# Reversed column order in the products that hold the weights in the array

## The reference

```python
for i in range(2):
    a = _rmsnorm(h, norm_mix[i])
    y = _mla(a, ...) if i == 0 else _swa_sinks(a, ...)       # each: h @ w_in, attention, @ w_o
    h = h + y
    h = h + _conv_ffn(_rmsnorm(h, norm_ffn[i]), ffn_w_in[i], ffn_conv_w[i], ffn_conv_b[i], ffn_w_out[i])
return _rmsnorm(h, final_norm)

def _conv_ffn(h, w_in, conv_w, conv_b, w_out):               # w_in 2048 x 11264, w_out 5632 x 2048
    u = h @ w_in
    c = conv_b + sum(shifted(u, j) * conv_w[j] for j in range(3))
    gate, val = jnp.split(c, 2, axis=-1)
    return (jax.nn.silu(gate) * val) @ w_out
```

## Time and profile before

| | value |
|---|---|
| median of three runs | 2016.89 us (2015.31 to 2018.02) |
| the profiled execution's own time | 2015.52 us |
| its span, first to last instruction | 2013.4 us |
| mean granted TensorE clock | 0.997 |
| PE busy | 1984.8 us, 99% |
| DVE busy | 1424.3 us, 71% |
| ACT busy | 988.0 us, 49% |
| from HBM | 364.94 MB, 185 GB/s in the mean |

### The profile page before, as it was taken

One profiled execution on the slowest core, in us unless ns is written; L12 is line 12 of the kernel. 1 busy time (PEld: TensorE's weight loads), 2 busy tenths in 40 slices (PEclk: granted clock), 3 DMA queues, 4 the chain that ended last, 5 costly groups with the idle time before them and its releaser, 6 DMA issues.

```text
span 2013.4 us, 33994 instructions
## 1 busy us (share of the span) xinstructions
PE 1984.8 (99%) x12104; PEld 1767.9 (88%) x12104; DVE 1424.3 (71%) x1964; ACT 988.0 (49%) x1159; POOL 146.3 (7%) x147
## 2 busy tenths in 40 slices
PE   8999999999999999999999999999999999999998
PEld 7898888888888888888899888888888888888887
DVE  7766687887787877554566668778787877855554
ACT  6456445555555554434355554555555555533332
POOL 1112220000000000110120004100000000001110
PEclk9999999999999999999999999999999999999999
DMA  7556555555555565556675335655556555555553
GB/s 280 160 195 157 180 197 190 192 181 197 191 185 177 192 202 189 188 179 202 191 242 174 126 127 168 199 192 183 179 193 201 188 180 199 185 197 189 189 188 115
DMA packets 103881, 374.48 MB, mean 186 GB/s; under 512 B 11547, under 2 KB 12124, under 8 KB 103548
## 3 DMA queue, kind: packets, MB, share of 16 engines
q1 hardware_dynamic: 101180, 362.55, 54.4%
q0 software_dynamic: 2624, 10.83, 2.1%
HBM read 364.94 MB, written 8.39 MB: 185 GB/s over the span
## 4 chain that ended last, share of the span: by engine, by line
PE 91%; DVE 4%; issue 0%; ACT 0%; DVEq 0%; ACTq 0%
PE ps L409 53%; PE ps L412 28%; PE ps L694 2%; PE ps L695 1%; PE ps L696 1%; DVE w_lo L1111 1%; DVE scores_b L1500 1%; PE ps L732 1%; PE ps L743 1%; PE ps L755 1%; PE ps L440 1%; PE ps L439 1%; PE ps L438 1%; DVE cv L1126 0%; PE ps L513 0%
## 5 line engine op out<-in xcount | busy, mean ns | idle before, releaser
L1111 DVE TENSOR_TENSOR w_lo<-raw,w_hi 128x1024 fp32r<-128x1024 f32 (+1 forms) x682 | 830.6, 1231 | 503.5 <-ACT w_hi L825 482.3
L825 ACT ACTIVATE w_hi<-raw 128x1024 fp32r<-128x1024 f32 (+1 forms) x682 | 715.2, 1055 | 792.3 <-PE ps L412 593.7
L409 PE MATMUL ps<-op_in,w_hi 128*128 128x512 f32 x2992 | 1028.2, 391 | 9.5 <-DVE w_lo L1111 9.5
L412 PE MATMUL ps<-op_in,w_lo 128*128 128x256 f32 x2992 | 813.0, 282 | 0.0
L409 PEld LDWEIGHTS ps<-op_in,w_hi 128*128 128x128 f32 x2992 | 549.7, 188 | 113.8 <-issue 8.4
L412 PEld LDWEIGHTS ps<-op_in,w_lo 128*128 128x128 f32 x2992 | 565.7, 189 | 15.7
L409 PE MATMUL ps<-op_ffn,w_hi 128*128 128x512 f32 x1408 | 486.2, 390 | 0.0
L412 PE MATMUL ps<-op_ffn,w_lo 128*128 128x256 f32 x1408 | 391.7, 282 | 0.0
L409 PEld LDWEIGHTS ps<-op_ffn,w_hi 128*128 128x128 f32 x1408 | 262.2, 188 | 53.0
L412 PEld LDWEIGHTS ps<-op_ffn,w_lo 128*128 128x128 f32 x1408 | 266.0, 189 | 2.7
L1616 POOL TENSOR_TENSOR cg<-h 128x1024 f32 (+1 forms) x15 | 43.2, 2877 | 1604.9 <-DVE h L1364 1454.3
(11 more groups left out here) (203 smaller groups left out, 1663.5 us busy)
## 6 DMA issues: line engine op xcount, KB each, us to landing
raw<-weights SPq DMA_DIRECT2D x666, 512.0 KB, 3.4
raw<-weights SPq DMA_DIRECT2D x16, 384.0 KB, 3.2
bias_rows<-brow POOLq DMA_DIRECT2D x1, 6144.0 KB, 36.7
win_bias<-bias_rows POOLq DMA_DIRECT2D x4, 1024.0 KB, 8.6
h<-xt SPq DMA_DIRECT2D x8, 256.0 KB, 7.7
x_tok<-x_rows SPq DMA_DIRECT2D x2, 1024.0 KB, 10.3
y<-yt SPq DMA_DIRECT2D x4, 512.0 KB, 4.0
par<-params SPq DMA_DIRECT2D x1, 352.0 KB, 11.5
```

The costliest lines, as they stand in the source:

```text
L409: return mm(ps[:, bank, 0:2 * T], whi, op, start=start, stop=stop)
L412: return mm(ps[:, bank, 0:T], wlo, op[:, 0, :], start=False, stop=False)
L825: f(w_hi[s][:, 0:cols], raw[s][:, 0:cols], ACT.Copy).then_inc(hi_ready, 1)
L1111: v.tensor_tensor(w_lo[s][:, 0:cols], raw[s][:, 0:cols], w_hi[s][:, 0:cols].bitcast(F32), ALU.subtract).then_inc(lo_ready, 1)
```

## The change

All products with stationary weights (L409 and L412, L513 to L515, L694 to L696) read the columns of their moving operand with a step of -1, from the last to the first, and write the PSUM columns with a step of -1 as well, so that each result lands where it did. In a wide product the two parts of the operand are taken as one run of 512 columns, and that run is reversed. Number, shape, order, buffers and waits of the instructions of every engine stay as they are; the line numbers behind L409 go up by one.

```diff
                 def high():
-                    return mm(ps[:, bank, 0:2 * T], whi, op, start=start, stop=stop)
+                    return mm(ps[:, bank, 0:2 * T][:, ::-1], whi, op.rearrange("p a t -> p (a t)")[:, ::-1],
+                              start=start, stop=stop)
 
                 def low():
-                    return mm(ps[:, bank, 0:T], wlo, op[:, 0, :], start=False, stop=False)
+                    return mm(ps[:, bank, 0:T][:, ::-1], wlo, op[:, 0, :][:, ::-1], start=False, stop=False)
...
-                            o = ps[:, b0 + m // 2, m % 2 * T:(m % 2 + 1) * T]
-                            mm(o, w_hi[s][:, w], x[:, 0, :], start=c == 0 and kt == 0 and m != 1, stop=False)
-                            mm(o, w_lo[s][:, w], x[:, 0, :], start=False, stop=False)
-                            z = mm(o, w_hi[s][:, w], x[:, 1, :], start=False, stop=c == 1 and kt == 1 and m != 0)
+                            o = ps[:, b0 + m // 2, m % 2 * T:(m % 2 + 1) * T][:, ::-1]
+                            mm(o, w_hi[s][:, w], x[:, 0, :][:, ::-1], start=c == 0 and kt == 0 and m != 1, stop=False)
+                            mm(o, w_lo[s][:, w], x[:, 0, :][:, ::-1], start=False, stop=False)
+                            z = mm(o, w_hi[s][:, w], x[:, 1, :][:, ::-1], start=False, stop=c == 1 and kt == 1 and m != 0)
...
-                    o = ps[:, bank + j // 2, j % 2 * T:(j % 2 + 1) * T]
+                    o = ps[:, bank + j // 2, j % 2 * T:(j % 2 + 1) * T][:, ::-1]
...
-                        mm(o, w_hi[s][:, w], op[:, kt0 + k, 0, :], start=first and k == 0 and j % 2 == 0, stop=False)
-                        mm(o, w_lo[s][:, w], op[:, kt0 + k, 0, :], start=False, stop=False)
-                        z = mm(o, w_hi[s][:, w], op[:, kt0 + k, 1, :], start=False, stop=last and k == 1 and j % 2 == 1)
+                        mm(o, w_hi[s][:, w], op[:, kt0 + k, 0, :][:, ::-1], start=first and k == 0 and j % 2 == 0, stop=False)
+                        mm(o, w_lo[s][:, w], op[:, kt0 + k, 0, :][:, ::-1], start=False, stop=False)
+                        z = mm(o, w_hi[s][:, w], op[:, kt0 + k, 1, :][:, ::-1], start=False, stop=last and k == 1 and j % 2 == 1)
```

## The result

The changed kernel takes 2037.82 us (median of 4 runs, 2036.15 to 2039.31), the kernel before 2016.2 us (4 runs, the profiled one among them): a ratio of 1.0103, interval 1.009 to 1.0115. It is 21.6 us slower. I had forecast no change, at 2016.5 us; the time lies within the range of 1990 to 2065 us and on the side of a rival.

A forecast was written before the change was run, and what follows sets the result against it. The prediction took PE (TensorE) as the bound, with 1850 of 2013.4 us in edited products. All four items summed to 0 on the profiled 2015.52 us; with the runs' median 1.4 us above, it forecast 2016.5 us, range 1990 to 2065.

The forecast's parts named there:

- no change: Whole kernel: the reversed products cost nothing more or less, about 2016.5 us, 2012 to 2021 in this case; chance 0.55.
- What bounds the kernel: PE, busy 99% of the span: any nanosecond added to or taken from an edited product is one of the program.
- Item 1: Moving operand of the edited products read downwards: taken as 0, since a jump of read address costs at most 1 ns.
- Item 2: PSUM written downwards by the edited products: taken as 0, between wide bounds of 5230 us loss and 45 us gain.
- Item 3: Distance between a PSUM write and the add on it, 256 columns instead of 512 within a wide tile: price 0.
- Item 4: Load of the next product's weights: unchanged, might hide some ns at 4848 + 1440 products, none at the wide ones.
- The doubled column: Rival: in reversed products each column is handled alone and takes twice its time, 3820 us in all; chance 0.15.
- The fixed price per product: Rival: each reversed product costs a few ns more, 2028 us at 1 ns, 2061 us at 4 ns; chance 0.15.
- Less stalling: Rival: weight loads and moving reads meet less in memory, 1971 us if all 4 ns go, 1994 at half; chance 0.15.
- the 4 ns besides the columns: Time a product of 256 columns holds beside its columns, 0.117 - 0.113 us; by 11136 products, 45 us of possible gain.

The follow-up runs named there:

- experiment 3: Kernel before, wide tiles read and written downwards, but the wide product takes its two halves in the usual order: 2036.39 us, ratio 1.0097.
- read_down: Kernel before, only the moving operand of both wide-tile products read downwards, PSUM written upwards: 2037.58 us, ratio 1.0103.
- write_down: Kernel before, only the PSUM outputs of both wide-tile products written downwards, operand read upwards: 2017.63 us, ratio 1.0001.
- halves_down: The run of experiment 3: kernel before, wide tiles downwards, the wide product's halves in the usual order: 2036.39 us, ratio 1.0097.
- experiment 6: Kernel before, all reads upwards, wide tiles take their weights 8 columns (32 bytes) further on: 2045.29 us, ratio 1.014.
- experiment 4: Kernel before, only the wide product of the wide tiles turned round, in operand and PSUM: 2046.41 us, ratio 1.0147.
- experiment 7: Kernel before, only the narrow product of the wide tiles turned round, in operand and PSUM: 2015.76 us, ratio 0.9993.
- up_off160: Kernel before, upward reads, operand tiles placed 128 bytes further on: 2018.51 us in one run, beside 2018.26 us for the kernel before.
- up_off0: Kernel before, upward reads, operand buffers at 0 instead of 32 modulo 128 bytes: 2046.29 us, ratio 1.0141.
- up_w32: The run of experiment 6: kernel before, upward reads, wide tiles' weights taken 32 bytes further on: 2045.29 us, ratio 1.014.
- low_down: The run of experiment 7: kernel before, only the narrow product of the wide tiles turned round: 2015.76 us, ratio 0.9993.

## Why the prediction was wrong, point by point

*What bounds the kernel* was right: each added ns of a wide tile came out in the span, and nothing hid it.

*Item 1, the downward read taken at 0*, is the step that failed. Its size is 4.3 ns a wide tile of `f0_out` and 1.1 ns a product of the narrow tiles, 20.1 us of the program from the 501st product on. I took the bound from L438, whose operand with a hole costs no more than one without. The jump is indeed free (experiment 3), but that row says nothing of a direction. It also compares mean durations, which the prediction itself had called latencies: L413 stood at 282 ns before and after, while its tile went from 346.8 to 351.1. In the runs the loss of the wide tiles came with the downward read alone (read_down 351.1 ns, write_down 346.8); in the narrow tiles read and write were not turned apart.

*Item 2, the downward write at 0*, was right, as write_down shows with 346.8 ns. The Trainium skill, PSUM — Partial Sum Buffer, Specifications (TRN2), warns of patterns that are not contiguous; by that run a step of -1 is none of them. *Item 3*, the distance between write and add at 0, was right too: write_down has the new distance at the old price, halves_down the old distance at the new price.

*Item 4* looked at the weight load only as a possible cover. Its place moves the price as much as anything done to the operand: 6.4 ns by 32 bytes (experiment 6). It gave no cover either: the narrow tiles, all of whose products might have been hidden, lost 1.1 ns a product.

*The rivals.* The doubled column (0.15) didn't happen. The fixed price per product (0.15, from 1 ns on, 2028 us and more) had sign and size: 21.6 us over 11136 products is 1.9 ns. Its mechanism did not hold, for experiment 4 turned fewer products and lost more. "Less stalling" (0.15) had the two parties that the runs point to, loads of weights and moving reads, and the wrong sign. Its bound of 45 us for a gain was not sound: the 4 ns besides the columns come from taking the narrow product at the 0.117 us of the narrow tiles. The wide tiles' own starts, 118.3 and 228.4 ns apart, would give 8 ns by the same sum, and as the split moves without a price (experiment 7), neither figure bounds anything. I had argued it down with two phases whose operands lie at different addresses and that have one price. That was no evidence: `op_in` and `op_ffn` both begin at 32 modulo 128 bytes, and a further step of 128 bytes moves the price by only 0.1 ns (up_off160, 346.9). The line of the code that sets this 32 is in the kernel before; a place so exact in a buffer layout was the hint that direction, too, would be felt. Had I given the meeting its weight, both signs would have been open, and no change would have deserved less than 0.55.

*What stays open.* That the price hangs on the place of both reads of TensorE is shown. That their distance decides rests on one pair, the distance 0 made in two ways (353.1 and 353.2 ns, the same split); the places could still count one by one. How the memory serves the two reads, which of them waits, why one product turned costs more than both, and why a downward read finds no good place, is not shown: the loads have 188 to 189 ns in the rows of the kernel before, of up_off0 and of up_w32 alike. The weights were read in one direction only; the opposite was not tried. Steps of 16 bytes were made by moving the weights alone, so there the weights' own place is not told apart from the distance. Even the best tile, 346.8 ns, may hold some such stalling; how much, no run shows.

## What to carry to other kernels

Where TensorE is the bound and each product has its own weight load, the place of the moving operand against the weights modulo 128 bytes is a size to tune: here it is worth up to 6.5 ns of 347 for upward reads, 1.9%, with the operand 32 bytes on as the best of five. Read upwards unless a measurement says otherwise; the direction of the write was free here. Judge such an edit by the distance of starts over hundreds of products, not by mean durations, and take two addresses as different places only if they differ modulo that period (32 and 160 had one price here). When a sum of small prices meets the difference of two spans, look where in the program the difference arises before you call it the whole: here 2 us of it lay in a stage that varies from run to run.

## What the runs showed of the hardware

- A moving operand read with a step of -1 took from 351.1 to 356.6 ns a wide tile at eight distances, upward ones 346.8 to 353.3 at five.
- PSUM written with a step of -1 took 346.8 ns a wide tile, as with a step of 1. An add to a column right behind the write of it, a distance of 1, stalled nothing in low_down (346.6 ns against 346.8).
- The place of the operand alone moved the price of a tile from 346.8 to 353.1 ns (32 bytes back) and that of a narrow product from 117.0 to 120.4.
- The place of the weight load alone moved the price of a tile from 346.8 to 353.2 ns (32 bytes) and 353.3 (16 bytes). The Trainium skill, TensorE: Matmul & The Clock Gate, Step-by-step: what each phase is for, says that loading the next weights takes no read bandwidth from the running matmul. If that is read as "the loads can lie anywhere", these runs do not agree; whether bandwidth is what is lost, or the load itself takes longer, they don't show.
- The price of a tile is the same to 0.1 ns in both layers: 346.8 ns in `f0_out` and in `f1_out` before, 351.1 in both after.
